# Inverse roots of the norms as exp(-ln/2) on ScalarE, and three reorderings, in a two-block transformer kernel

## What is computed

```python
def rms_norm(x, g):
    y = x * lax.rsqrt(jnp.mean(x * x, axis=-1, keepdims=True) + NORM_EPS)
    return y * g

# block 1
mem_n = rmsnorm(mem, g_mem)
x = x + mixer(rmsnorm(x, g_mix), ...)            # gated linear attention (a norm per head) + block-sparse attention, two sigmoid gates
x = x + memory_attention(rmsnorm(x, g_cross), mem_n, ...)    # 4 heads against the memory
x = x + hier_moe(rmsnorm(x, g_moe), ...)         # 32 experts, silu(xb @ w_gate) * (xb @ w_up) @ w_down
x = rmsnorm(x, g_final)
# block 2: two layers of
h = rms_norm(x, g_attn); proj = h @ w_in
o_diff = rms_norm(diff_attention(...), subln)    # two softmaxes, a norm per head
o_sb = stick_breaking_attention(...)             # log-sigmoid (softplus) and exp of 8 heads
x = x + (sigmoid(g1) * (o_diff @ w_o_diff) + sigmoid(g2) * (o_sb @ w_o_sb)) @ w_out
x = x + (silu(gate) * up) @ w_ffn_out            # gate, up of rms_norm(x, g_ffn) @ w_ffn_in, hidden width 2816
# and a last rms_norm
```

## Time and profile before

| | |
|---|---|
| median of 3 runs | 1500.06 us (1498.95 to 1500.63) |
| profiled execution | 1496.68 us, span 1494.9 us |
| PE busy | 1361.7 us, 91% |
| DVE busy | 789.5 us, 53% |
| ACT busy | 594.9 us, 40% |
| HBM read | 372.42 MB, 250 GB/s over the span |

### The profile page before, as it was taken

The page is one execution under the profiler, slowest core; times in us unless marked ns, Lnnn a source line. Parts: engine busy times, 40 slices in busy tenths (PEclk is TensorE's granted clock), DMA queues, the critical chain, the costliest instruction groups (busy, mean ns, idle before and its releaser), DMA issues.

```text
span 1494.9 us, 23605 instructions
## 1 busy us (share of the span) xinstructions
PE 1361.7 (91%) x10389; PEld 1140.1 (76%) x10389; DVE 789.5 (53%) x1110; ACT 594.9 (40%) x743; POOL 14.7 (1%) x32
## 2 busy tenths in 40 slices
PE   8999999997777678677899999999999999999998
PEld 6898898744333334333789899999999989999986
DVE  6656877411111011100788887666467688865653
ACT  4554555311000000000546765543434586544433
POOL 0000000000000000000010000000001000000000
PEclk9999999998889888989999999999999999999999
DMA  9553458899999999999853445556536434555640
GB/s 310 186 174 114 146 177 349 336 427 427 427 427 427 427 426 426 427 426 424 296 190 114 170 155 184 170 171 223 199 115 197 168 121 162 170 194 181 230 170 28
DMA packets 117407, 377.13 MB, mean 252 GB/s; under 512 B 8216, under 2 KB 53624, under 8 KB 104760
## 3 DMA queue, kind: packets, MB, share of 16 engines
q1 hardware_dynamic: 115879, 371.52, 65.1%
q0 software_dynamic: 1424, 4.08, 1.1%
HBM read 372.42 MB, written 1.06 MB: 250 GB/s over the span
## 4 chain that ended last, share of the span: by engine, by line
PE 62%; DMA 21%; DVE 10%; ACT 4%; issue 1%; SPq 1%; POOL 0%; ACTq 0%; DVEq 0%
PE bank L656 29%; DMA ring<-in_w_exp_up 11%; PE bank L932 5%; PE bank L708 4%; PE bank L1303 4%; PE bank L1297 4%; DVE parts L1844 4%; PE bank L1105 3%; PE bank L678 3%; DMA tail_hn<-in_w_exp_up 3%; DMA SZ<-in_w_exp_up 3%; DMA ring<-in_w_exp_down 3%; PE bank L1135 2%; PE bank L1058 2%; DVE SQ L2020 1%
## 5 line engine op out<-in xcount | busy, mean ns | idle before, releaser
L1844 DVE TENSOR_TENSOR parts<-ring,parts 128x2048 fp32r<-128x2048 f32 x155 | 349.6, 2288 | 99.0 <-ACT parts L1393 98.2
L656 PE MATMUL bank<-hnr,parts 128*128 128x256 f32 x2784 | 339.4, 284 | 0.4 <-DVE parts L1844 0.4
L656 PEld LDWEIGHTS bank<-hnr,parts 128*128 128x128 f32 x2784 | 335.6, 192 | 1.8 <-DVE parts L1844 0.7
L1393 ACT ACTIVATE parts<-ring 128x2048 fp32r<-128x2048 f32 x152 | 282.4, 1905 | 94.8 <-PE bank L1303 29.2
L656 PE MATMUL bank<-SKr,parts 128*128 128x256 f32 x1824 | 226.8, 284 | 2.3 <-DVE parts L1844 2.2
L656 PEld LDWEIGHTS bank<-SKr,parts 128*128 128x128 f32 x1824 | 220.9, 192 | 4.0 <-DVE parts L1844 2.1
L1105 PE MATMUL bank<-ring,TMP 128*32 128x512 f32 x576 | 86.7, 756 | 47.1 <-DMA ring<-in_w_exp_up 47.1
L2244 DVE COPY KV<-bank 128x256 f32<-128x256 f32 x16 | 6.8, 425 | 217.8 <-PE bank L1085 217.8
L1105 PEld LDWEIGHTS bank<-ring,TMP 128*32 128x32 f32 x576 | 22.6, 134 | 104.2 <-issue 89.5
L1569 ACT ACTIVATE TMP<-bank 128x512 f32<-128x512 f32 x15 | 9.0, 597 | 158.9 <-PE bank L1058 158.9
L932 PE MATMUL bank<-Gr,parts 128*128 128x256 f32 x576 | 69.8, 283 | 2.2 <-DVE Gr L2027 2.2
(11 more groups left out here) (401 smaller groups left out, 1880.0 us busy)
## 6 DMA issues: line engine op xcount, KB each, us to landing
ring<-in_w_in SPq DMA_DIRECT2D x60, 1024.0 KB, 7.4
ring<-in_w_ffn_in SPq DMA_DIRECT2D x44, 1024.0 KB, 6.9
ring<-in_w_exp_gate SPq DMA_DIRECT2D x18, 2048.0 KB, 38.8
ring<-in_w_exp_up SPq DMA_DIRECT2D x18, 2048.0 KB, 43.4
ring<-in_w_exp_down SPq DMA_DIRECT2D x18, 2048.0 KB, 39.0
ring<-in_w_ffn_out SPq DMA_DIRECT2D x20, 1024.0 KB, 6.1
...
```

Of the source, the lines that this page charges most:

```text
L656: m = mm(b(name)[:, T * half:T * half + T], part(chunk, ws)[:, k, P * mt:P * mt + P], src[xs][:, k, :], start=k == 0 and i == 0, stop=k == ...
L1393: A(parts[:, 2 * (r % 2), 2048 * i:2048 * i + 2048], ring[:, CHUNK[chunk][0], 2048 * i:2048 * i + 2048], ACT.Copy).then_inc(high_made, 1)
L1844: v.tensor_tensor(parts[:, 2 * (r % 2) + 1, at], ring[:, CHUNK[chunk][0], at], parts[:, 2 * (r % 2), at].bitcast(F32), ALU.subtract).then_ ...
```

## The change

1. **Roots.** `inverse_root` takes ln of the scaled sum (plus epsilon) and then exp(-0.5 times it), both on ACT, the second waiting for the first. All reciprocals of norms on DVE go. The one root that isn't inverted (`both_weight`) is exp(+0.5 ln). Ln and Exp come from one table set, which is loaded by name where a stretch of them begins; Sigmoid and Silu are loaded ahead of their first use. ACT_TABLE_LOAD stands 15 times in ACT's order, where it stood 44 times. Semaphores that passed the inverted roots on go as well, and DVE's wait for the memory's root moves behind the three additions of squares.
2. **Fillers.** PE runs five plain float32 matmuls of 128x256 on bank 7 behind the bucket matmul.
3. **Scores of the memory.** PE waits for cq0, scores heads 0 and 1, waits for cq1, scores heads 2 and 3.
4. **Tail of layer 0.** The tail weights are split, by ACT and DVE, behind the first chunk of the down projection, into `tail_first` (the tile `hnr`), and multiplied in three passes with the split hidden values.

```diff
                       for which in range(2)]
+        tail_first = [hnr[:, which, :, :].rearrange("p k n -> p (k n)").rearrange("p (k n) -> p k n", k=2) for which in range(2)]
         gain_row = tail_hn[:, 2048:3072]
...
 
+                width = math.prod(moving.shape[1:])
                 for _ in range(n):
-                    mm(ps[bank][:, :], stationary, moving, start=True, stop=True)
+                    mm(ps[bank][:, 0:width], stationary, moving, start=True, stop=True)
 
...
             fin(m, "bucket")
+            filler(7, 5, TMP[:, 0:128], TMP[:, 0:256])
             split_by_turns("ckv_k", mem_parts, ["kc0", "kc1"], None)
...
                 room(pe, "mr")
-                pe.wait_ge(mem_root_ready, 1)
+                emptied(pe, "n_mem")
                 for tb in range(TB):
...
             emptied(pe, "cq0")
-            emptied(pe, "cq1")
             emptied(pe, "kc0")
             emptied(pe, "kc1")
-            for h in range(4):
-                cross_scores(h)
+            cross_scores(0)
+            cross_scores(1)
+            emptied(pe, "cq1")
+            cross_scores(2)
+            cross_scores(3)
 
...
                 room(pe, "nr" + x)
-                pe.wait_ge(attn_root_ready, l + 1)
+                emptied(pe, "n_attn" + x)
                 for tb in range(TB):
...
                 if l + 1 == LAYERS:
-                    pe.wait_ge(tail_split, 1)
+                    pe.wait_ge(tail_split, LAYERS)
                     pe.wait_ge(hid_split, 11 * (l + 1))
...
                     break
-                pe.wait_ge(tail_landed, 16 * (l + 1))
-                pe.wait_ge(hid_scaled, 11 * (l + 1))
+                pe.wait_ge(tail_split, 1)
+                pe.wait_ge(hid_split, 11 * (l + 1))
                 for mt in range(8):
                     for kk in range(2):
-                        m = mm(b(f"fo{mt // 2}{x}")[:, T * (mt % 2):T * (mt % 2) + T], tail_w[:, kk, P * mt:P * mt + P],
-                               hid_raw[10 % 3][:, kk, :], start=False, stop=kk == 1, skip_group_check=True)
+                        for ws, xs in PASSES:
+                            m = mm(b(f"fo{mt // 2}{x}")[:, T * (mt % 2):T * (mt % 2) + T], tail_first[ws][:, kk, P * mt:P * mt + P],
+                                   hid_parts[xs][:, 20 + kk, :], start=False, stop=kk == 1 and (ws, xs) == PASSES[2],
+                                   skip_group_check=True)
                     if mt % 2 == 1:
...
 
+            def logs_and_exps():
+                act.preload_act_table_set("natural_log_exp_and_others")
+
+            def inverse_root(dst, src, bias, scale):
+                link(A(dst, src, ACT.Ln, bias=bias, scale=scale))
+                return A(dst, dst, ACT.Exp, scale=-0.5)
+
+            logs_and_exps()
             act.wait_ge(eps_ready, 1)
...
                 to = attn_root if name.startswith("n_attn") else ffn_root if name.startswith("n_ffn") else final_root if name == "n_final" else root
-                freed(A(to, b(name)[:, 0:T], ACT.Sqrt, bias=eps2_col if name == "n_attn.0" else eps_col, scale=1.0 / D), name)
+                made = inverse_root(to, b(name)[:, 0:T], eps2_col if name == "n_attn.0" else eps_col, 1.0 / D)
+                freed(made, name)
 
...
                     full(act, name)
-                    freed(A(hroot[:, 2 * i:2 * i + 2, :], b(name)[:, :].rearrange("p (a b) -> p a b", b=T), ACT.Sqrt,
-                            bias=eps_col, scale=1.0 / P), name)
+                    freed(inverse_root(hroot[:, 2 * i:2 * i + 2, :], b(name)[:, :].rearrange("p (a b) -> p a b", b=T),
+                                       eps_col, 1.0 / P), name)
 
...
             act.wait_ge(weight_ready, 1)
-            A(both_weight, both_weight, ACT.Sqrt, bias=eps_col).then_inc(weight_root, 1)
+            link(A(both_weight, both_weight, ACT.Ln, bias=eps_col))
+            A(both_weight, both_weight, ACT.Exp, scale=0.5).then_inc(weight_root, 1)
             for j in range(4):
...
             full(act, "n_mem")
-            freed(A(mem_root, b("n_mem")[:, 0:T], ACT.Sqrt, bias=eps_col, scale=1.0 / D), "n_mem")
+            freed(inverse_root(mem_root, b("n_mem")[:, 0:T], eps_col, 1.0 / D), "n_mem")
             norm_squares("n_mix", xres, [f"xt{j}" for j in range(4)])
...
             take("r1", two(rg, 1), func=ACT.Silu)
+            logs_and_exps()
             high("km")
...
                     causal_exp(h + 2, [prob[h % 2]])
+                if h + 2 == 7:
+                    act.preload_act_table(ACT.Sigmoid)
                 take(("zg2", "zg3", "zm0", "zm1", "zm2", "zm3")[h - 2], two(z1, h) if h < 4 else two(z2, h - 4))
...
             sigmoid("zm3", z2)
+            logs_and_exps()
             high("out0")
...
 
-            A(sm[:, 93:94], eps_col, ACT.Exp)
             cross_exp(0)
...
             full(act, "n_moe")
-            freed(A(tok_root, b("n_moe")[:, 0:TB], ACT.Sqrt, bias=eps_col, scale=1.0 / D), "n_moe")
-            act.wait_ge(tok_root_ready, 1)
+            freed(inverse_root(tok_root, b("n_moe")[:, 0:TB], eps_col, 1.0 / D), "n_moe")
+            emptied(act, "n_moe")
             for j in range(4):
...
             A(ex2, dm, ACT.Exp).then_inc(route_exp, 1)
+            act.preload_act_table(ACT.Silu)
 
...
                         act_pair(o, q * PAIRS + p, q * (PAIRS + 1) + p)
+            logs_and_exps()
             act.wait_ge(weight_root, 1)
...
                         high("proj_diff" + x, [h - 5])
+                act.preload_act_table(ACT.Sigmoid)
                 gate_sigmoid("ga3" + x, ga, 0)
...
                 gate_sigmoid("gb3" + x, gb, 8)
+                logs_and_exps()
                 high("out0" + x)
...
                 norm_root("n_ffn" + x)
+                act.preload_act_table(ACT.Silu)
                 for j in range(11):
...
                             freed(A(x_last[:, HALF * i:HALF * i + HALF], b(f"xt{i}{x}")[:, :], ACT.Copy), f"xt{i}{x}")
+                logs_and_exps()
                 for c in range(5 if l + 1 < LAYERS else 3):
...
                         high(SPLIT[SPLIT.index(f"down{c}{x}") + 2])
+                    if c == 0 and l == 0:
+                        act.wait_ge(tail_landed, 16)
+                        full(act, f"fu10{x}")
+                        A(tail_first[0], tail_w, ACT.Copy).then_inc(tail_high, 1)
             act.wait_ge(tail_landed, 16 * LAYERS)
...
             A(tail_parts[0], tail_w, ACT.Copy).then_inc(tail_high, 1)
-            A(sm[:, 93:94], eps_col, ACT.Sqrt)
-
             def last_square(i):
...
                 act.wait_ge(mean_made, tb + 1)
-                A(tok_root[:, tb:tb + 1], sq_sum[:, 2 * tb + 1:2 * tb + 2], ACT.Sqrt, bias=sq_mean[:, tb:tb + 1],
-                  scale=1.0 / D).then_inc(last_root, 1)
+                inverse_root(tok_root[:, tb:tb + 1], sq_sum[:, 2 * tb + 1:2 * tb + 2], sq_mean[:, tb:tb + 1],
+                             1.0 / D).then_inc(tok_root_ready, 1)
 
             def last_first_half(tb):
-                act.wait_ge(tok_root_ready, 2 + tb)
+                act.wait_ge(tok_root_ready, 1 + tb)
                 act.wait_ge(y_gained, tb + 1)
...
                 emptied(dve, name)
-                link(v.reciprocal(root, root))
                 for k in range(KT):
...
                 take(f"xt{j}", two(xres, j))
-            emptied(dve, "n_mem")
-            v.reciprocal(mem_root, mem_root).then_inc(mem_root_ready, 1)
             for j in range(1, 4):
                 add_squares("n_mix", j)
-            dve.wait_ge(mem_root_ready, 1)
+            emptied(dve, "n_mem")
             take_scaled("kc0", two(kc, 0), over_tiles(mem_root))
...
                 emptied(dve, names[h // 2])
-                link(v.reciprocal(hroot[:, h, :], hroot[:, h, :]))
                 return v.scalar_tensor_tensor(o[:, h, :], o[:, h, :], col, hroot[:, h, :], ALU.mult, ALU.mult)
...
             emptied(dve, "n_cross")
-            link(v.reciprocal(root, root))
             take_scaled("cq0", two(qc, 0), over_tiles(root))
...
             emptied(dve, "n_moe")
-            v.reciprocal(tok_root, tok_root).then_inc(tok_root_ready, 1)
-            dve.wait_ge(tok_root_ready, 1)
             full(dve, "route")
...
                 emptied(dve, name)
-                v.reciprocal(attn_root, attn_root).then_inc(attn_root_ready, 1)
-                dve.wait_ge(attn_root_ready, l + 1)
                 by_attn = over_tiles(attn_root)
...
                     emptied(dve, "n_final")
-                    link(v.reciprocal(final_root, final_root))
                 diff_norm(1)
...
                 emptied(dve, "n_ffn" + x)
-                link(v.reciprocal(ffn_root, ffn_root))
                 by_root = over_tiles(ffn_root)
...
                         low(SPLIT[SPLIT.index(f"down{c}{x}") + 2])
-            dve.wait_ge(tail_high, 1)
+                    if c == 0 and l == 0:
+                        dve.wait_ge(tail_high, 1)
```

(10 more changed lines are left out.)

5 lines of the change are left out of this document (2 added, 3 removed).

## The result

The changed kernel takes 1481.7 us (median of 4 runs, 1480.5 to 1484.56), the kernel before 1500.35 us in the same comparison: ratio 0.9879, 95% interval 0.9861 to 0.9896. A second comparison later (experiment e9) gave 1484.29 against 1499.69, ratio 0.9898, interval 0.9881 to 0.9914. The prediction was 1484.6 us, a gain of 15.4; the medians gained 18.65 us in the first comparison and 15.4 in the second, and the two profiled executions differ by 15.8 us (span 1494.9 to 1479.1).

A forecast was written before the change was run, and what follows sets the result against it. PE's work, busy 91% of the span, plus the gaps others open in it was taken as the bound. The terms summed to 15.4 us, taken from 1500.06 to give 1484.6 us; range 1480.8 to 1492.4.

The forecast's parts named there:

- start: Start up to the mixer's squares: missing memory reciprocal and fillers that keep PE's clock full gain 1.5 us.
- mixer: Mixer: softmax gaps and one low part, behind table loads and reciprocals, close; gain 5.0 us.
- memory: Attention to the memory: PE scores heads 0 and 1 while DVE makes cq1; gain 1.0 us.
- experts: Route and experts: 0 us, the gain made ahead living through the DMA-bound stage.
- layer 0: Layer 0's projections: a reciprocal and a load go ahead of low-part gaps; gain 0.4 us.
- stick-breaking: Stick-breaking, both layers, with output projection: gaps behind table loads and reciprocals close; gain 7.0 us.
- tail: Layer 0's tail: 48 faster matmul records replace 32, 1.15 us, of which 0.3 comes back; gain 0.85 us.
- end: End of the kernel: ACT's one root becomes Ln and Exp ahead of its output half; loss 0.35 us.
- Rival (b): Mixer and stick-breaking: freed waits return as the next ones, half of 12 us lost; 1490.6 us, chance 0.10.
- Rival (c): Experts: changed rhythm lowers PE's mean clock, so PE becomes the bound; 1509 us, chance 0.02.
- (d): Table loads: sets reloaded on every switch between Ln and Exp, so loads stay; about 1494 us, chance 0.01.
- the rule: Experts: the weight stream waits for PE at its start, so every later fill moves along, PE 7.5 us earlier.

The follow-up runs named there:

- e9: The changed kernel again, unaltered, beside the kernel before in five rounds; 1484.29 us against 1499.69, ratio 0.9898.
- e1: The changed kernel without the five filler matmuls; its end came 1.46 us later than the changed kernel's.
- e2: The kernel before with the five filler matmuls alone added; its execution was 2.6 us longer than the profile of the kernel before.
- e3: The kernel before with Ln and Exp for roots and the changed kernel's 15 table loads, DVE's reciprocals kept, no reorderings; span 1488.8 us, 6.1 shorter.
- e4: The changed kernel with Exp and Ln in two table sets again, 38 loads instead of 15; 10.8 us later at the end than the changed kernel.
- e8: The changed kernel with PE waiting for both cq0 and cq1 before the memory's first score; PE lost 1.07 us there.
- e5: The changed kernel with 7.7 us of useless matmuls on PE ahead of the mixer's output projection; 8.84 us later at the end.
- e10: The changed kernel with two more reorderings, at the memory's attention and the mixer's gate projection; 1480.66 us, ratio to the kernel before 0.987.
- e7: The changed kernel with layer 0's tail in plain float32 again, without its split; PE 3.53 us later behind the tail, which began 2.81 later.

## Why the prediction was right, point by point

**The way of counting** held. Each gap plus 0.16 us, summed over those ended by a chain that the change shortens, gave 15.4 us; the profiles gave 15.8. That the two are so near is in part luck. The terms missed by +0.7 (start), +0.3 (mixer), +0.05 (memory), -1.0 (experts), +0.2 (layer 0), +0.5 (stick-breaking), -0.4 (tail) and +0.1 (end), which largely cancel, and start, mixer, memory and stick-breaking all came out above their upper bounds (1.7, 5.3, 1.0, 7.2), the mixer's and the memory's barely. (The terms' upper bounds add up to 18.0 us, not 17.7.) Rival (b), that freed waits return, is out for the mixer and the stick-breaking stage: no line of the after profile's waits is new. Rival (c) is out, since PEclk is 0.89 from 292 to 700 us in both kernels, and (d), since the trace has 15 loads.

**Start: right in kind, too small.** 1.5 was predicted, with 1.7 as the cap of both effects; it was 2.2. e1 and e2 give the parts: 0.2 for the fillers alone, 1.2 to 1.3 for the rest alone, 2.2 for both. The cap failed, since I took 1.74 us of reciprocal as all that DVE could gain. The first release of L678 came 0.26 us earlier too (14.43 to 14.17), and with it all of DVE's queue; that much lies within the spread of the start, and without it the sum of squares starts 1.64 us earlier, inside the cap. The other 0.27 us came ahead of the next projections at 46.77, where DVE had a second reciprocal of 128x256 (L1806, 39.02 to 40.77) ahead of their scaled input. PE's wait there was too short to be printed, so the sum had no term for it; e3, which still has this reciprocal, doesn't gain these 0.27 us.

**Mixer and memory's attention: right** (5.3 and 1.05 for 5.0 and 1.0). e4 shows that the loads alone make a gap of 2.1 at the first head, e3 that removing them alone leaves the three other gaps as they were: these are the reciprocals'. e8 shows that the memory's gap belongs to the order of the waits. No run took the reciprocals out alone; that the three gaps are theirs rests on their being there in e3 and gone in the changed kernel.

On the drain that the Trainium skill adds to each switch (page "ScalarE: Activation LUTs", section "What ACT_TABLE_LOAD costs"): e4's rows put the next activation at 141.46, behind a load that starts at 140.17 and takes 1.28, and the two loads (135.89 and 140.17) and the added Exps make the wait 2.12 us, near the 2.2 of the rows alone. No run here shows the drain.

**Experts: the rule held, the zero didn't quite.** e5's 7.88 us went through as 7.87. In the changed kernel the first fills are issued 7.53 us earlier (246.51 to 238.98; 6.5 were predicted) and those of the down weights 8.60 earlier (271.58 to 262.98), and the last up weights are still taken 8.61 us earlier (708.01 to 699.40). The loss comes in the last matmuls of the stage. The 32 that take the last down weights, changed kernel, its stretch, and the kernel before:

```profile
707.29 5.11 PE L1139 MATMUL bank<-ring,KV 128*32 128x512 f32 x32 [1.05 <-issue]
...
706.90:710.30 3.40, 3.01 (x16) 0.50 1.03 389
```

```profile
715.91 1.92 PE L1135 MATMUL bank<-ring,KV 128*32 128x512 f32 x16 [1.05 <-issue]
718.02 1.92 PE L1135 MATMUL bank<-ring,KV 128*32 128x512 f32 x16 [0.19 <-DMA ring<-in_w_exp_down]
```

They take 5.11 us with the clock at its lower level for 3.4 us, and 4.03 us with it at the upper one, so 1.07 of the gain goes here: it is the granted clock's, and not the stream's. Most of what e9 lost against the first profile of the same kernel, 2.2 us up to the end of this stage, is the clock's too: 1.4 of it arose between 266 and 271 us, where e9's clock is 0.50 for 6.8 us and the first profile's for 3.4. Why the clock falls there isn't known; no wait stands ahead of it (last section).

**Stick-breaking: the sum near, one attribution wrong.** 7.5 us for 7.0. The prediction put L932's two gaps (2.5 us) down to three reciprocals of 5.2 us ahead of them. In e3 all three are still there, and both gaps are gone. In e4 the reciprocals are gone and the loads are back (38 of the 44), and there is no gap either. So removing either the loads or the reciprocals is enough. What the step lacked was that the same gap may be claimed by two removed costs; I counted it once, which is why the sum is right.

**Layer 0's projections: inside its bounds.** 0.57 us against 0.4. Its larger gap was 1.05, 0.44, 1.37, 0.77 and 0.99 us in before, after, e5, e9 and e10. In all five profiles DVE first waits for a transfer (tail_hn<-G, 0.5 to 2.8 us) ahead of that low part, so it seems to move with the landing and not with the change; no run held the transfer fixed.

**Tail: mis-sized.** 0.45 us (0.56 in e7) instead of 0.85. PE's part was right (32 by 0.216 against 48 by 0.120 us, first to last start 6.7 and 5.7 us). What comes back behind it was taken as 0.3 and is 0.6 to 0.7.

**End: right** within 0.1 us. Two rows of ACT, Ln and Exp, stand where one stood:

```profile
1473.59 0.30 ACT L1352 ACTIVATE sm<-sm 128x1 f32<-128x1 f32 x1
1473.91 0.20 ACT L1353 ACTIVATE sm<-sm 128x1 f32<-128x1 f32 x1
1474.02 1.32 ACT L1788 ACTIVATE G<-G,sm 128x512 f32<-128x512 f32 x2
```

**Still open.** The medians differed by 18.65 us in one comparison and 15.4 in the other, the profiles by 15.8. The profile of before (1496.68) is below all its four runs of the first comparison, and both profiles lack the clock fall behind the experts that seven of twelve show. That fits, but clock and waits of the unprofiled runs aren't seen, so it isn't shown.
